# Diffusion layer on one core: the modulation block merged with the first head's projections, done by quarters

## The reference, cut to what matters

```python
sh1, sc1, g1, sh2, sc2, g2 = split((silu(c) @ w_ada + b_ada), 6)      # and the same for c_ctx
h  = x * (1 + sc1) + sh1          # modulate; context tokens with their own shift and scale
proj = h @ w_in                   # per head: dq dk dv | mq mk mv mo, and 32 gate columns
dq, dk, dv, mqk, mv, mo, mg = split(proj)
mqk = silu(depthwise_conv5(mqk))
d_lat = rms(softmax(q1 k1') v - lam * softmax(q2 k2') v)     # 8 heads, differential attention
m_lat = rms(mlstm(mq, mk, mv, gates, both directions)) * sigmoid(mo)   # 8 heads
x = layer_norm(a * x + g1 * (concat(d_lat, m_lat) @ w_out))
x = layer_norm(a * x + g2 * peer_ffn(x * (1 + sc2) + sh2))
```

## Time and profile before

| | us |
|---|---|
| median of 3 runs (4144.89 to 4154.94) | 4148.83 |
| the profiled execution | 4151.25 |
| its span | 4149.5 |
| PE busy | 3824.9 (92%) |
| DVE busy | 2850.5 (69%) |
| ACT, POOL busy | 1144.1, 1104.8 |
| mean granted clock of PE, share of full | 0.962 |

### The profile page before, as it was taken

The page is one execution under the profiler, slowest core; times in us unless marked ns, Lnnn a source line. Parts: engine busy times, 40 slices in busy tenths (PEclk is TensorE's granted clock), DMA queues, the critical chain, the costliest instruction groups (busy, mean ns, idle before and its releaser), DMA issues. The chain is left out here.

```text
span 4149.5 us, 59995 instructions
## 1 busy us (share of the span) xinstructions
PE 3824.9 (92%) x21024; PEld 3370.8 (81%) x21024; DVE 2850.5 (69%) x4092; ACT 1144.1 (28%) x1777; POOL 1104.8 (27%) x926
## 2 busy tenths in 40 slices
PE   7799999999998598895879999999999999999997
PEld 3387877877787486443779999999999999999996
DVE  0246555555644433599878888888888888888897
ACT  0112122222222222111933232233233233233231
POOL 0353433343343253302021221221221221221220
PEclk9899999999999698997989999999999999999999
DMA  8233333333332532221478888888888888888995
GB/s 316 92 100 109 121 101 105 115 114 103 114 121 86 182 136 85 91 71 71 183 260 309 305 314 307 322 307 315 319 309 312 324 306 318 320 306 306 333 339 206
DMA packets 340406, 887.28 MB, mean 214 GB/s; under 512 B 115712, under 2 KB 118208, under 8 KB 276352
## 3 DMA queue, kind: packets, MB, share of 16 engines
q1 hardware_dynamic: 291968, 546.84, 38.6%
q0 software_dynamic: 46080, 335.56, 21.5%
q10 hardware_dynamic: 2304, 4.20, 0.3%
HBM read 849.63 MB, written 35.79 MB: 213 GB/s over the span
## 5 line engine op out<-in xcount | busy, mean ns | idle before, releaser
L1154 PE MATMUL PS<-xh,UH 128*128 128x352 f32 x2048 | 664.4, 324 | 26.4 <-POOL UL L1140 17.6
L1765 PE MATMUL PS<-AL,VH 128*128 128x352 f32 x2048 | 669.6, 327 | 0.0
L1156 PE MATMUL PS<-xh,UL 128*128 128x352 f32 x2048 | 662.6, 324 | 0.0
L1155 PE MATMUL PS<-xl,UH 128*128 128x352 f32 x2048 | 658.6, 322 | 0.0
L447 PE MATMUL PS<-hH,WH 128*128 128x512 f32 (+1 forms) x1408 | 523.2, 372 | 52.8 <-POOL WL L792 45.6
L449 PE MATMUL PS<-hH,WL 128*128 128x512 f32 (+1 forms) x1408 | 501.7, 356 | 0.0
L448 PE MATMUL PS<-hL,WH 128*128 128x512 f32 (+1 forms) x1408 | 501.1, 356 | 0.0
L1717 POOL DMA_INDIRECT Ub<-peer_u,stage x160 | 203.3, 1271 | 938.8 <-DVE Ub L1895 903.9
L1154 PEld LDWEIGHTS PS<-xh,UH 128*128 128x128 f32 x2048 | 384.9, 188 | 33.2 <-issue 17.8
L1155 PEld LDWEIGHTS PS<-xl,UH 128*128 128x128 f32 x2048 | 388.1, 189 | 0.0
L1765 PEld LDWEIGHTS PS<-AL,VH 128*128 128x128 f32 x2048 | 386.8, 189 | 0.0
(11 more groups left out here) (313 smaller groups left out, 7026.0 us busy)
## 6 DMA issues: line engine op xcount, KB each, us to landing
UR<-peer_ut SPq DMA_DIRECT2D x128, 1024.0 KB, 7.1
VR<-peer_v SPq DMA_DIRECT2D x256, 512.0 KB, 6.5
AW<-wada SPq DMA_DIRECT2D x256, 256.0 KB, 3.0
WR<-wseq SPq DMA_DIRECT2D x224, 256.0 KB, 2.6
wr<-wada SPq DMA_DIRECT2D x8, 4096.0 KB, 14.4
gates_dram<-GS SPq DMA_DIRECT2D x11, 2048.0 KB, 6.3
GB<-gates_dram SPq DMA_DIRECT2D x64, 352.0 KB, 6.3
oR<-wout SPq DMA_DIRECT2D x32, 512.0 KB, 3.9
```

Of the source, the lines that this page charges most:

```text
L1154: pe.matmul(dst, UH[:, j % 2, k, :], xh[:, k, :], start=(k == 0), stop=False)
L1155: pe.matmul(dst, UH[:, j % 2, k, :], xl[:, k, :], start=False, stop=False)
L1156: last = pe.matmul(dst, UL[:, j % 2, k, :], xh[:, k, :], start=False, stop=(k == KT - 1))
L1765: pe.matmul(low, VH[:, slot, j, cols], AL[:, :, b, :], start=False, stop=False)
```

## The change

It takes the first block apart and puts it into the heads' block.

- Modulation by quarters of the input width. A chunk of `w_ada` is now four 1 MB units in four slots (`unit`), in the order shift chunk, scale chunk, so that after each two chunks a quarter of the input (4 of 16 tiles) can be modulated.
- Column groups. The stationary operand of a chunk's matmul is the 2 columns `silc[:, :, k]` and no longer 128; row tile k writes to PSUM rows 32*(k % 3) and on, so that three sums stand in one bank in three groups of 32 columns of the array. The small matmuls of `mod_columns` add the three with `picks`. The gates' matmuls are put in three groups in the same way, kept in `G3`, and added and placed by four matmuls with `sel`: the two directions in rows 0 to 7 and 32 to 39, with no way through DRAM.
- Projections between. The tiles mq, mk, mo of head 0 are made quarter by quarter as input quarters become ready; mv follows, then dq. `hL` is made by DVE, a tile at a time, and no longer by POOL.
- The gates' rows are 40 x 768 and no longer 8 x 1536; head 0's three convolutions stand behind the scans.
- Pieces in pairs. `AW` has 8 places, a DMA loads two pieces (512 KB) and there are 16 issues per head at new positions in `AFTER`.
- In `stage_b` of ACT `exps(h, 1)` and `keep_wt(h, 0)` now stand ahead of `silu_q`.
- Space: `qq`, `rawdk` and `on` are gone; the rotary step works in place in `rawdq` and `kk`, and `on` is `hn`.

```diff
+GRP = 3
+GR = 40
...
+            hT = over("hT", "mst", [P, KT, T])
...
+            wr = over("wr", "AW", [P, 4, QK, CHUNK])
...
+                    def unit(n):
+                        c, kq = n // 4, n % 4
+                        if n >= 4:
+                            sp.wait_ge(s_unit, n - 3)
+                        sp.dma_start(wr[:, kq, :, :], wv4[:, QK * kq:QK * kq + QK, c // 2 + 4 * (c % 2), :]).then_inc(s_aw[kq], 16)
+                    def inputs(q):
+                        ks = slice(QK * q, QK * q + QK)
+                        sp.dma_start(hT[:, ks, 0:SEQ], xv[:, ks, :]).then_inc(s_x[q % 2], 16)
+                        sp.dma_start(hT[:, ks, SEQ:T], cxv[:, ks, :]).then_inc(s_x[q % 2], 16)
+                    def first_weights(i):
+                        if i >= WBUF:
+                            sp.wait_ge(pe_qtr, i - WBUF + 1)
+                        sp.dma_start(WR[:, i % WBUF, :, :], wseq[4 * FIRST[i % 3] + i // 3]).then_inc(w_loaded[i % WBUF], 16)
+                    for n in range(4):
+                        unit(n)
...
+                    inputs(0)
+                    FIRST = (TILE["mq"], TILE["mk"], TILE["mo"])
+                    WEIGHTS_AFTER = (7, 7, 7, 7, 15, 15, 19, 23, 23, 27, 31, 31)
+                    for n in range(4, UNITS):
+                        unit(n)
+                        if n % 8 == 3:
+                            inputs(n // 8)
+                        for i, m in enumerate(WEIGHTS_AFTER):
+                            if m == n:
+                                first_weights(i)
...
-                        sp.dma_start(AW[:, i % 4, :], wv4[:, i % KT, SH_CHUNKS + 2 * h + i // KT, :]).then_inc(s_aw[i % 4], 16)
...
+                    def ada_pieces(h, d):
+                        sp.wait_ge(s_aused, PIECES * h + 2 * d + 2)
+                        sp.dma_start(AW[:, 2 * (d % ADA_SLOTS):2 * (d % ADA_SLOTS) + 2, :],
+                                     wv4[:, 2 * d % KT:2 * d % KT + 2, SH_CHUNKS + 2 * h + 2 * d // KT, :]).then_inc(s_aw[d % ADA_SLOTS], 16)
+                    AFTER = (1, 3, 5, 6, 10, 11, 12, 13, 14, 16, 18, 20, 22, 25, 26, 26)
...
+                    def ada_chunk(c):
+                        pe.wait_ge(s_ada_ev, c)
+                        for k in range(KT):
+                            if k % QK == 0:
+                                pe.wait_ge(s_aw[k // QK], 16 * c + 16)
+                            j = 32 * (k % GRP)
+                            last = pe.matmul(PS[j:j + 2, 0, :], silc[:, :, k], wr[:, k // QK, k % QK, :], start=(k < GRP), stop=(k >= KT - GRP))
+                            if k % QK == QK - 1:
+                                last.then_inc(s_unit, 1)
+                    def mod_columns(q):
+                        pe.wait_ge(s_ada_ev, 2 * q + 2)
+                        for a in range(2):
+                            for i in range(4):
+                                o = 16 * q + 8 * a + 2 * i
+                                last = pe.matmul(PS[:, 1, o:o + 2], R[0:66, a, i * P:(i + 1) * P], picks[0:66, 0:2], start=True, stop=True)
+                        last.then_inc(s_modT, 1)
+                    def gates(q):
+                        for k in range(QK * q, QK * q + QK):
+                            pe.wait_ge(s_mod, k + 1)
+                            j = 32 * (k % GRP)
+                            first, end = k < GRP, k >= KT - GRP
+                            pe.matmul(PS[j:j + 32, 6, :], wg[:, k, :], hT[:, k, 0:SEQ], start=first, stop=end)
+                            last = pe.matmul(PS[j:j + 32, 7, 0:CTX], wg[:, k, :], hT[:, k, SEQ:T], start=first, stop=end)
+                        last.then_inc(s_gate_pe, 1)
+                    def first_part(i, q, parts):
...
+                                pe.wait_ge(s_hl, kk_ + 1)
...
+                    ada_chunk(0); ada_chunk(1); mod_columns(0)
+                    ada_chunk(2); gates(0); first_qtr(0, 0); first_qtr(1, 0)
+                    ada_chunk(3); mod_columns(1); first_qtr(2, 0)
+                    ada_chunk(4); gates(1); first_qtr(0, 1); first_qtr(1, 1)
+                    ada_chunk(5); mod_columns(2); first_qtr(2, 1)
+                    ada_chunk(6); gates(2); first_qtr(0, 2); first_qtr(1, 2); first_qtr(2, 2)
+                    ada_chunk(7); mod_columns(3); gates(3)
+                    pe.wait_ge(s_gate_ev, 1)
+                    for g, (dst, t0, t1) in ((1, (PS[0:GR, 0, :], 0, SEQ)), (1, (PS[0:GR, 7, CTX:2 * CTX], SEQ, T)),
+                                             (0, (PS[0:GR, 6, :], 0, SEQ)), (0, (PS[0:GR, 7, 0:CTX], SEQ, T))):
+                        last = pe.matmul(dst, sel[:, g, :], G3[:, t0:t1], start=True, stop=True)
+                    last.then_inc(s_gsel, 1)
+                    for t in range(3):
+                        first_qtr(t, 3)
+                    pe.wait_ge(s_abs, 1)
+                    for q in range(4):
+                        if q == 0:
+                            pe.wait_ge(act_evac, 2)
+                        first_part(3 * 4 + q, q, [(B(0), 0, SEQ), CTXP])
+                    pe.wait_ge(act_evac, 4)
...
-                        exps(h, 0)
-                        if proj: silu_q(g)
-                        exps(h, 1)
+                        exps(h, 0); exps(h, 1)
                         keep_wt(h, 0)
-                        if proj: keep_mv(g)
+                        if proj:
+                            silu_q(g); keep_mv(g)
...
+                    for q in range(4):
+                        for a in range(2):
+                            act.wait_ge(s_unit, 4 * (2 * q + a) + 4)
+                            if q:
+                                act.wait_ge(s_modT, q)
+                            act.activation(R[0:66, a, :], PS[0:66, 0, :], ACT.Copy).then_inc(s_ada_ev, 1)
+                        for k in range(QK * q, QK * q + QK):
+                            act.wait_ge(s_mod, k + 1)
+                            act.activation(hH[:, k, :], hT[:, k, :], ACT.Copy).then_inc(s_hh, 1)
+                    act.wait_ge(s_gate_pe, 4)
+                    act.activation(G3[:, 0:SEQ], PS[0:32 * GRP, 6, :], ACT.Copy)
+                    act.activation(G3[:, SEQ:T], PS[0:32 * GRP, 7, 0:CTX], ACT.Copy).then_inc(s_gate_ev, 1)
...
+                    keep_mq(0, 3, 10); keep_mk(0, 4, 11); keep_mo(0, 5, 12)
...
+                    keep_mv(0, 16); silu_k(0); silu_q(0); keep_v(0)
...
+                    for q in range(4):
...
+                        dve.wait_ge(s_x[q % 2], 32 * (q // 2) + (32 if q % 2 else 16 * 7))
+                        for k in range(QK * q, QK * q + QK):
+                            for a, (t0, t1) in enumerate(((0, SEQ), (SEQ, T))):
+                                last = dve.tensor_scalar(hT[:, k, t0:t1], hT[:, k, t0:t1], mods[:, KT + k, a:a + 1],
+                                                         mods[:, k, a:a + 1], ALU.mult, ALU.add)
+                            last.then_inc(s_mod, 1)
+                        for k in range(QK * q, QK * q + QK):
+                            dve.wait_ge(s_hh, k + 1)
+                            dve.tensor_tensor(hL[:, k, :], hT[:, k, :], hH[:, k, :].bitcast(f32), ALU.subtract).then_inc(s_hl, 1)
+                    dve.wait_ge(s_gsel, 1)
...
+                    dve.wait_ge(s_tab, 49)
+                    conv_k(0); conv_kc(0); conv_q(0)
```

More of the change, by code:

```diff
@@ L45 @@
 SH_CHUNKS = 2 * D // CHUNK
+UNITS = 4 * SH_CHUNKS
+GRP = 3
+GR = 40
 OUK = 2
@@ L49 @@
 PIECES = 2 * KT
+ADA_SLOTS = 4
 OUT_CHUNKS = D // CHUNK
@@ L281, in program @@
         pe_o, dve_dout = sem("at_out_turned"), sem("at_out_kept")
-        s_aw = [sem(f"ada_piece_loaded{i}") for i in range(4)]
         s_aused = sem("ada_pieces_added")
@@ L479, in m2 @@
                         for d in range(2):
-                            last = pe.matmul(B(3 + d), selH[:], Mrow[:, d, :], start=True, stop=True)
+                            r = slice(32 * d, 32 * d + H)
+                            last = pe.matmul(B(3 + d), selH[r, :], Mrow[r, :], start=True, stop=True)
                         last.then_inc(pe_m2, 1)
@@ L979, in stage_b @@
                         att_norm(h)
+                    dve.memset(PS[0:32 * GRP, 0, :], 0.0)
+                    dve.memset(sel[:], 0.0)
+                    dve.wait_ge(s_small, 32)
+                    dve.memset(picks[:], 0.0)
+                    dve.drain()
+                    dve.tensor_reduce(picks[0:32 * GRP, :], ident[0:32 * GRP, 0:32 * GRP].rearrange("p (j r) -> p r j", j=GRP), AX.X, ALU.add)
+                    dve.drain().then_inc(s_pick, 1)
+                    for g in range(2):
+                        for d in range(2):
+                            src = 8 * g + 16 * d
+                            dve.tensor_copy(sel[:, g, 32 * d:32 * d + H], picks[0:32 * GRP, src:src + H])
@@ new lines, in _ @@
+                    for s in (ml_stored, at_stored):
+                        dve.drain().then_inc(s, 1)
+                    for _ in range(2 * ADA_SLOTS):
```

(17 more changed lines are left out.)

401 lines of the change are left out of this document (169 added, 232 removed).

## The result

The changed kernel takes 4005.94 us (median, 4003.76 to 4014.54) where the kernel before took 4148.22 in the same comparison: a ratio of 0.9659, interval 0.9640 to 0.9678. The prediction was 4012.

What follows compares the result with a forecast made beforehand. It took a DMA-paced front and PE's waits in the heads as what the change could shorten: 4151.25 us less 94 (front), 35 (heads) and 7.5 (last head) is 4014.8, less 2.4 to the median 4012; range 3968 to 4068.

Steps and rivals of the forecast that it cites:

- Front: Program start to dk of head 0: 180 us in place of 274.1, a gain of 94, with DMA setting the pace.
- the last unit: Front: the last 1 MB unit of w_ada arrives at 119.5 us.
- PE term: Front: PE needs 5.2 us per chunk of w_ada, 41 us for all, if the three column groups run at once.
- PE fits under it, 88 in 119: Front: chunks, turning, gates and projection quarters take PE 88 us within 119 us of transfers, so DMA sets the pace.
- No overlap: Rival, front: column groups run one after another, PE sets the pace, front 228.5 us, gain 45.6, time 4061; chance 0.18.
- The two rivals with a front slowed by SP's queue or by PE's clock: Front: SP's queue, gain 70 us, time 4036, chance 0.14; slow PE clock, front 400 us, time 4233, slower chance 0.04.
- First wait in the heads: PE's wait at pv(h, 0) for keep_wt goes: 2.83 us of wait, 6 us a head with line 550 and slow clock.
- Second wait: Heads: the split-weights wait goes, a 3.9 us wait for WT at pv(h, 2) replaces it; net loss 0 to 1 us.
- POOL's contention: Heads, chain to WT: busy POOL delays DVE on the shared SBUF path, bounds 0 and 3 us a head, taken as 1.5.
- The rival with both waits gone: Heads: DVE gets ahead by not waiting for pieces, 12 us a head in place of 5, time 3963; chance 0.12.
- Last head: DVE's 15.47 us wait for a held-back piece, with PE behind it, is relieved; the norm comes 7.5 us earlier.
- Heads and last head together: Seven heads at 5 us each, 35 us, and 7.5 us in the last head.

Runs made afterwards that it cites:

- e_half_ada: Changed kernel with the DMAs of every second chunk of w_ada cut to 64 KB; one run, dk of head 0 at 171.3 us, 7.0 earlier.
- e_front_only: Changed kernel with ACT's order and the pieces as before, only the merged front left; 4037.51 us, ratio 0.9749.
- e_max: Changed kernel with DVE's maxima(h, 3) moved before pieces 10 to 12, ACT's order unchanged; 3976.68 us, ratio 0.9579.
- e_best: Changed kernel with maxima(h, 3) first, second-chunk pieces moved earlier, and keep_wt(h, 2) between exps(h, 3) and keep_mo; 3954.81 us, ratio 0.9552.
- e_wt_max: Changed kernel with keep_wt(h, 2) before exps(h, 3) on ACT and maxima(h, 3) before pieces 10 to 12 on DVE; 3975.32 us, ratio 0.9603.

## Why the prediction was right, step by step

**Front, 94 us predicted, 95.8 measured.** The rate (388 GB/s against some 385), the last unit (119.5 against 122) and dk of head 0 (180 against 178.3) hold. Its PE term was mis-sized: the eight chunks took 55.5 us of PE, not 41. The overlap was taken rightly: a chunk with its data there is 5.31 us (5.2 predicted). What the term left out is in chunks 0 to 2, 9.1 to 9.2 us each, where PE waited for units. The granted clock was 0.51 from 25 to 30 us, at the start of chunk 1, and a unit that came alone took four rounds of 0.43 us for its 4 row tiles, 1.88 us in all, for a quarter of a chunk. This cost nothing only because DMA's pace hid it, and e_half_ada shows by how little, 7 us. The step "PE fits under it, 88 in 119" should have read 100 in 124.

The Trainium skill, "TensorE: Matmul & The Clock Gate", Part 3, states 2.38 times for three column groups. The trace gives 2.62 for a chunk at full clock, with 2 stationary columns in float32, and the measurement decides. The changes of tiling mode, which the prediction could not price, show no gap at this place: chunk 7's first matmul starts at 118.04, 0.32 us after the full-array matmul before it, where those follow each other every 0.23.

**No overlap.** That rival priced the front at 228.5; with the groups taken away it was 225.3. It was wrong of the kernel and right in its sum. The two rivals with a front slowed by SP's queue or by PE's clock did not come either: the DMA rate has only two short dips up to 122 us, and the granted clock was 0.92.

**First wait in the heads, 6 us.** Right: 5.9, 5.7 and 6.0 on three different kernels.

**Second wait, 0 to 1 us lost.** Right in kind, mis-sized. The wait for split weights went, one at `pv(h, 2)` took its place, and PE's own way there was 15.5 us (15.6 predicted). But the wait is 6.1, not 3.9, and the pairs cost 2.0 us a head. The term that failed is POOL's contention: I took 1.5 from a range of 0 to 3, and it is 3.5 (21.5 us against 18.0 with the same instructions and POOL idle up to `nm` of `maxima(1, 3)`). DVE lost it in four places of head 1. A product of `conv_k` took 1.52 us and the first piece 1.75, where 0.75 is usual, and each ended some 0.55 after a subtraction of POOL. `rz` of line 934, 0.16 us with POOL idle, took 0.99 and ended at 433.75, as POOL's subtraction did (433.74). `nm` of line 928, 0.17 us, took 1.11 and ended at 442.38, and POOL's subtraction at 442.35.

The Trainium skill, "SBUF — State Buffer", section on the two separate sides, says that the shared pair is locked for the whole instruction, between POOL and DVE work with two inputs in SBUF or in a faster mode. The trace agrees: `rz` and `nm` ran to the end of POOL's, and line 926, which reads PSUM, took 1.75 us in both kernels.

The period still fell by 4.8 us (147.0 to 142.3), near the 5 predicted, because 1.1 us a head came with the front (e_front_only), for which the prediction had 0. That part is luck.

**What the prediction did not see** is that this wait was a matter of order. It read the chain from `maxima(2)` to `WT` as 18 us "with no gap" and as given. Three pieces, 3.4 us, stood in it only because DVE's program put them ahead of `maxima(3)`, and moving them brought 5.9 us a head. The rival with both waits gone had 3963; e_max, two changed lines away, took 3976.7 with 1.9 us a head of the wait left, and e_best 3954.8.

**Last head, 7.5 us.** From head 6 to head 7 the old pieces take 142.9 us against 137.8, so 5.1. The other waits there, for the norm and the rotary step, stayed.

**Heads and last head together**: 42.5 predicted, 37.8 measured (133.6 - 95.8). The rest behind them was to cost the same; it took 10.4 us less in this pair of profiles, and that covered the shortfall. Without it the 4012 would have been some 4 low instead of 6 high: the total is right partly by luck.

## What to carry to other kernels

When a wait goes, work out the arrival time of the next one from both chains, and then ask of each link whether data or only program order put it there; moving filler work out from between two links was here worth more than the buffers and the DMA order. A transfer plan and a work order belong together: pairs with eight slots cost time in one order and carried the gain in the other. A wait on TensorE can cost more than its length, and no one factor holds: 2.9 us at `pv(h, 0)` cost 5.9, while in e_wt_max 2.9 us a head at `turn(h, 3)` left PE's busy time at 800.29 us, where e_best has 799.58. Compare the busy time of the same instructions.

## What the runs showed of the hardware

- Three column groups with 2 stationary columns, float32, 512 moving columns: a chunk of 32 instructions in 5.31 us instead of 13.90 at a granted clock of 1.00; all 256 in 55.5 us of PE instead of 115.8, waits for data not counted.
- A wait of 2.9 us on PE in every head cost 5.9 us. In the changed kernel matmuls still took 0.63 us, 3.6 us after the end of the wait of 6.08 us, where 0.39 is usual; the granted clock from 443 to 453 us was 0.50, the lower of its two levels (order of time, start and length):

```profile
450.53 0.63 PE L375 MATMUL PS<-hH,WL 128*128 128x512 f32 x1
```

- DVE instructions on 128 x 1 and 128 x 2 elements took 0.99 and 1.11 us beside a POOL subtraction instead of 0.16 and 0.17.
- One core drew about 387 GB/s in most slices of 110 us.
